# Six or five matmuls a weight tile in an fp32-accurate decoder step, on one Trainium2 core

## The reference, cut to what matters

```python
bg, cg, xv = jnp.split(h @ w_in, 3, axis=-1)              # layer 0: 1024 -> 3*1024
conv, new_hist = causal_dwconv(cg * xv, hist, conv_w)
y = (bg * conv) @ w_out                                   # 1024 -> 1024
...
gconv, new_hist = causal_dwconv(h @ w_gate, hist, conv_w) # ConvFFN of each layer: 1024 -> 2816, twice
y = (jax.nn.silu(gconv + conv_b) * (h @ w_up)) @ w_down   # 2816 -> 1024
...
p = (h @ w_qkv).reshape(b, t, N_GROUPS, 3, H_SLOT, HEAD_DIM)   # layer 1: 1024 -> 4608
```

## Time and profile before

| | |
|---|---|
| three runs | 1483.51, 1487.76, 1491.68 us; median 1487.76 us |
| the profiled execution | 1491.81 us, of which 1490.3 us are the span of the trace |
| granted TensorE clock, mean over the span | 0.962 |
| busy: TensorE, weight loads, VectorE, ScalarE | 95%, 90%, 52%, 33% of the span |
| matmuls | 10995 |

### The profile page before, as it was taken

The page is one execution under the profiler, slowest core; times in us unless marked ns, Lnnn a source line. Parts: engine busy times, 40 slices in busy tenths (PEclk is TensorE's granted clock), DMA queues, the critical chain, the costliest instruction groups (busy, mean ns, idle before and its releaser), DMA issues.

```text
span 1490.3 us, 28043 instructions
## 1 busy us (share of the span) xinstructions
PE 1417.3 (95%) x10995; PEld 1342.2 (90%) x10995; DVE 778.9 (52%) x1236; ACT 487.7 (33%) x779; POOL 21.1 (1%) x50
## 2 busy tenths in 40 slices
PE   5999999999999999999989999776999999999998
PEld 5999999999999999988878888644499999999998
DVE  5655656565565333354454544667176555664223
ACT  3222334343433222333333333211153433332111
POOL 0000000000000000000000000000000000000000
PEclk9999999999999999999999999855899999999999
DMA  5254446544444444451340341397064445345331
GB/s 162 86 173 132 142 140 196 154 153 136 123 150 140 145 149 127 147 161 58 95 152 28 91 125 52 87 248 198 25 196 143 131 125 166 122 132 179 111 95 58
DMA packets 241729, 195.01 MB, mean 131 GB/s; under 512 B 6825, under 2 KB 229081, under 8 KB 240514
## 3 DMA queue, kind: packets, MB, share of 16 engines
q1 hardware_dynamic: 226976, 128.88, 30.9%
q0 software_dynamic: 1792, 54.43, 10.1%
q10 hardware_dynamic: 12906, 10.92, 2.4%
HBM read 186.58 MB, written 65.21 MB: 169 GB/s over the span
## 4 chain that ended last, share of the span: by engine, by line
PE 86%; DVE 5%; issue 3%; ACT 2%; DMA 2%; SPq 1%; ACTq 1%; DVEq 0%
PE acc L1267 74%; PE N L1256 2%; PE M L1432 2%; PE acc L1576 2%; DMA big<-new_q 1%; PE N L1461 1%; PE acc L1295 1%; DVE big L1130 1%; PE M L1256 1%; DVE big L1069 1%; ACT big L732 1%; PE M L1453 1%; PE M L1449 1%; ACT big L719 1%; SPq L458 1%
## 5 line engine op out<-in xcount | busy, mean ns | idle before, releaser
L1267 PE MATMUL acc<-hh,wh 128*128 128x260 f32 x2320 | 480.1, 288 | 1.0 <-issue 1.0
L1267 PE MATMUL acc<-hh,wl 128*128 128x260 f32 x2320 | 467.0, 283 | 0.0
L1267 PE MATMUL acc<-hl,wh 128*128 128x260 f32 x2320 | 466.7, 283 | 0.0
L573 ACT ACTIVATE wh<-wraw 128x1024 fp32r<-128x1024 f32 x212 | 222.8, 1051 | 500.2 <-PE acc L1267 486.2
L1267 PEld LDWEIGHTS acc<-hh,wh 128*128 128x128 f32 x2320 | 359.3, 189 | 7.0 <-issue 1.3
L1267 PEld LDWEIGHTS acc<-hh,wl 128*128 128x128 f32 x2320 | 357.5, 188 | 0.0
L1267 PEld LDWEIGHTS acc<-hl,wh 128*128 128x128 f32 x2320 | 356.9, 188 | 0.0
L857 DVE TENSOR_TENSOR wl<-wraw,wh 128x1024 fp32r<-128x1024 f32 x212 | 257.4, 1214 | 177.1 <-ACT wh L573 168.9
L1267 PE MATMUL acc<-yh,wh 128*128 128x260 f32 x864 | 175.2, 284 | 3.0 <-DVEq L891 2.0
L1267 PE MATMUL acc<-yh,wl 128*128 128x260 f32 x864 | 174.5, 283 | 0.0
L1267 PE MATMUL acc<-yl,wh 128*128 128x260 f32 x864 | 174.2, 283 | 0.0
(11 more groups left out here) (182 smaller groups left out, 1162.1 us busy)
## 6 DMA issues: line engine op xcount, KB each, us to landing
out_dram<-in_cache_kv_d_dram POOLq DMA_DIRECT2D x24, 1364.0 KB, 6.2
wraw<-in_ffn_w_gate_dram SPq DMA_DIRECT2D x44, 512.0 KB, 3.8
wraw<-in_ffn_w_up_dram SPq DMA_DIRECT2D x44, 512.0 KB, 3.9
wraw<-in_attn_w_qkv_dram SPq DMA_DIRECT2D x36, 512.0 KB, 4.8
out_dram<-in_cache_kv_d_dram POOLq DMA_DIRECT2D x8, 2044.0 KB, 8.1
wraw<-in_ffn_w_down_dram SPq DMA_DIRECT2D x32, 448.0 KB, 3.7
wraw<-in_sc_w_in_dram SPq DMA_DIRECT2D x24, 512.0 KB, 3.8
wraw<-in_ffn_w_down_dram SPq DMA_DIRECT2D x16, 512.0 KB, 3.9
```

The source lines that it names most:

```text
L573: nc.scalar.activation(wh[c % 2][:, 0:k], wraw[:, c % 4, 0:k], ACT.Copy).then_inc(hi_done, 1)
L1267: ins = T.matmul(acc[:, par, h2, 0:HALF], w[c % 2][:, k, :], a[:, k0 + k, h2, :], start=(first and k == 0 and n == 0), stop=(last and k == ...
```

## The change

The two halves of tokens become unequal: A has 264 tokens, B has 256. For each weight tile five matmuls stand in place of six: wh·xh and wh·xl over A (264 columns each, both into bank 0), then one of 512 columns in which wh meets the high and the low part of B's activations one behind the other (into bank 1: its columns 0 to 255 collect the high product, 256 to 511 the low one), then wl·xh over A (264) and over B (256, added to columns 0 to 255 of bank 1). For that `hh` and `hl` are laid into one tensor `hhl` [128, 2, 8, 520] and `yh`, `yl` into `yhl`. All columns together stay 1560.

Bank 1 then holds two results for B. At each readout ScalarE copies the second one (256 columns) from PSUM into the new buffer `lo` (`keep_lo`, in `step`, ahead of the split), and VectorE adds it to the first in place in PSUM (`joined`), waits for that addition, and then reads the tile as one run of 520 tokens across the two banks (`tokens`). In S_QKV and the other stages a few readouts that were made for two halves become one of 520.

```diff
+        def tokens(two):
+            return two.rearrange("p h n -> p (h n)")[:, C0:C0 + TT]
...
+            def keep_lo(two, st, it, t):
+                act.wait_ge(acc_free, st.tile(it, t) + 2)
+                nc.scalar.activation(lo[:], two[:, 1, BB:2 * BB], ACT.Copy).then_inc(lo_kept, 1)
...
             def step(st, it, c, last=False):
                 g = st.chunk(it, c)
                 act.wait_ge(chunk_used, g + 1)
+                if st is S_DN0 or st is S_DN1:
+                    if c % 3 == 2:
+                        keep_lo(acc[:, (c // 3) % 2], st, it, c // 3)
+                elif st is S_IN and it == 0 and c == 2:
+                    keep_lo(M[:], st, it, c)
+                else:
+                    keep_lo(acc[:, c % 2], st, it, c)
...
             def finish(pair):
                 act.wait_ge(chunk_used, S_QKV.chunk(pair, 8) + 1)
+                keep_lo(acc[:, 0], S_QKV, pair, 8)
                 split_hi(S_QKV, pair + 1, 0)
...
+            def joined(two, st, it, t):
+                dve.wait_ge(lo_kept, st.tile(it, t) + 1)
+                ch.after(V.tensor_tensor(two[:, 1, 0:BB], two[:, 1, 0:BB], lo[:], ALU.add))
+                return tokens(two)
...
-                V.tensor_tensor(xm, acc[:, par, :, 0:HALF], xm, ALU.add).then_inc(x_ready, 1)
+                V.tensor_tensor(xm, joined(acc[:, par], st, it, m % 4), xm, ALU.add).then_inc(x_ready, 1)
...
-                    V.tensor_tensor(dst, src[:, :, 0:HALF], r[:], ALU.mult).then_inc(acc_free, 1)
+                    V.tensor_tensor(dst, joined(src, S_IN, it, k), r[:], ALU.mult).then_inc(acc_free, 1)
...
-                        V.tensor_tensor(u_prompt, acc[:, 0, :, 0:HP], prompt(r), ALU.mult)
-                        V.tensor_tensor(u_new, acc[:, 0, :, HP:HALF], sample(r), ALU.mult).then_inc(u_ready, 1)
+                        a = joined(acc[:, 0], gu, it, 2 * i)
+                        V.tensor_tensor(u_prompt, prompt(a), prompt(r), ALU.mult)
+                        V.tensor_tensor(u_new, sample(a), sample(r), ALU.mult).then_inc(u_ready, 1)
...
-                        ch.after(V.tensor_tensor(y32[:], acc[:, 1, :, 0:HALF], t1[:], ALU.mult))
+                        ch.after(V.tensor_tensor(y32[:], joined(acc[:, 1], gu, it, 2 * i + 1), t1[:], ALU.mult))
...
-                a = acc[:, c % 2]
+                a = joined(acc[:, c % 2], S_QKV, pair, c)
...
+            def tile_step(dst, w, a, k, first, last):
+                T.matmul(dst[:, 0, C0:512], w[0], a[:, 0, k, 0:BA], start=first, stop=False)
+                T.matmul(dst[:, 0, C0:512], w[0], a[:, 1, k, 0:BA], start=False, stop=False)
+                T.matmul(dst[:, 1, 0:2 * BB].rearrange("p (t n) -> p t n", t=2), w[0], a[:, :, k, BA:TT],
+                         start=first, stop=False)
+                T.matmul(dst[:, 0, C0:512], w[1], a[:, 0, k, 0:BA], start=False, stop=last)
+                return T.matmul(dst[:, 1, 0:BB], w[1], a[:, 0, k, BA:TT], start=False, stop=last)
...
-                    for n, (w, a) in enumerate(((wh, xh), (wh, xl), (wl, xh))):
-                        for h2 in range(2):
-                            ins = T.matmul(acc[:, par, h2, 0:HALF], w[c % 2][:, k, :], a[:, k0 + k, h2, :],
-                                           start=(first and k == 0 and n == 0),
-                                           stop=(last and k == nk - 1 and n == 2))
+                    ins = tile_step(acc[:, par], (wh[c % 2][:, k, :], wl[c % 2][:, k, :]), a, k0 + k,
+                                    first and k == 0, last and k == nk - 1)
```

More of the change, by code:

```diff
@@ L29 @@
 NS = 8
-HALF = 260
-HP = SEQ // 2
-HS = NS // 2
+TT = SEQ + NS
+BB = 256
+BA = TT - BB
+C0 = 512 - BA
 FF = 2816
@@ L1232, in _ @@
                     gained(3, m, m + 3 * DK)
+            ch.end(2)
             ch.begin()
@@ L1236, in _ @@
             ffn(1, S_GU1, S_DN1, DK + FK, 4 * DK, None, 2)
-            for j in range(2):
-                last = V.tensor_copy(xs_c[:, :, j * HS:(j + 1) * HS], x[:, :, j, HP:HALF])
-            last.then_inc(fin_xs, 1)
+            V.tensor_copy(xs_c, x[:, :, SEQ:TT]).then_inc(fin_xs, 1)
             for t in range(4):
@@ L1277, in mean_square @@
                 pe.wait_ge(ssq_ready, (norm + 1) * DK + 1)
-                for h2 in range(2):
-                    ins = T.matmul(N[:, h2, 0:HALF], rms_ones[:], ssq[:, h2, :], start=True, stop=True)
-                ins.then_inc(ms_ready, 1)
+                T.matmul(N[:, 0, C0:512], rms_ones[:], ssq[:, 0:BA], start=True, stop=True)
+                T.matmul(N[:, 1, 0:BB], rms_ones[:], ssq[:, BA:TT], start=True, stop=True).then_inc(ms_ready, 1)
             def first_chunk(norm):
@@ L1288, in first_chunk, with k_step @@
                 return {k: (lambda k=k: at(k)) for k in range(DK)}
-            def k_step(dst, c, k, xh, xl, first, last):
-                for n, (w, a) in enumerate(((wh, xh), (wh, xl), (wl, xh))):
-                    for h2 in range(2):
-                        ins = T.matmul(dst[:, h2, 0:HALF], w[c % 2][:, k, :], a[:, k, h2, :],
-                                       start=(first and n == 0), stop=(last and n == 2))
-                return ins
+            def k_step(dst, c, k, a, first, last):
+                return tile_step(dst, (wh[c % 2][:, k, :], wl[c % 2][:, k, :]), a, k, first, last)
             pe.wait_ge(pool_set, 6)
@@ L1400, in ffn @@
                     free_acc(gu, 0, c)
-                    products(gu, 0, c, c % 2, DK, hh, hl, 0, True, True, first_chunk(norm) if c == 0 else None)
+                    products(gu, 0, c, c % 2, DK, hhl, 0, True, True, first_chunk(norm) if c == 0 else None)
                 with pe.Fori(1, FK // 2) as it:
@@ L1459, in head_sums @@
                 pe.wait_ge(qsq_ready, pair * 6 + (i + 1))
-                for h2 in range(2):
-                    ins = T.matmul(N[:, h2, 0:HALF], head_ones[:], sq[:, h2, :], start=True, stop=True)
-                ins.then_inc(qms_ready, 1)
+                T.matmul(N[:, 0, C0:512], head_ones[:], sq[:, 0:BA], start=True, stop=True)
+                T.matmul(N[:, 1, 0:BB], head_ones[:], sq[:, BA:TT], start=True, stop=True).then_inc(qms_ready, 1)
             def project(pair, attend):
@@ L1498, in project @@
                         pe.wait_ge(kvt_dve, pair * 4)
-                    products(S_QKV, pair, c, c % 2, DK, hh, hl, 0, True, True, ins)
+                    products(S_QKV, pair, c, c % 2, DK, hhl, 0, True, True, ins)
             def finish(pair):
@@ L1590, in _ @@
                     free_acc(S_WO, it, c, d=1 if c == 0 else 2)
-                    products(S_WO, it, c, c % 2, NP_, yh_r, yl_r, 0, True, True)
+                    products(S_WO, it, c, c % 2, NP_, yhl, 0, True, True)
             ffn(1, S_GU1, S_DN1, DK + FK + NP_ + 1, 3)
```

163 lines of the change are left out of this document (80 added, 83 removed).

## The result

The changed kernel took 1498.55 us (median of 13 runs, 1495.53 to 1502.83), the kernel before 1488.53 us (13 runs on the same chip, 1483.51 to 1491.68): a ratio of 1.0072 [1.0058, 1.0086]. It is 10.0 us slower; the forecast was 6.8 us faster. The range held the time, but the direction was the rival's, "the extra goes by column".

What follows compares the result with a forecast made beforehand. TensorE's issue distance, 120.14 ns per matmul start, was taken as the bound. A gain of 17.7 us less 10.9 us of costs made −6.8 us: 1491.81 becomes 1485.0 (1481.0 for the median); range 1462 to 1500.

Steps and rivals of the forecast that it cites:

- the extra goes by column: Rival on TensorE: the extra time goes mostly by column, 2.5 ns saved a tile; +7.1 us, 1494.9; chance 0.22.
- fixed part per instruction: TensorE: each matmul carries 11.8 ns beyond its columns, so five instead of six save 11.8 ns a weight tile.
- the three readings: Why 260 columns take 120.14 ns: fixed per instruction, by column, or weight-load floor; 11.8, 2.5 or 24 ns saved a tile.
- The floor of the load: Rival: the weight load sets the 120 ns, the long matmul costs 216; 24 ns saved a tile, −25 us; chance 0.10.
- the rival of the dearer long matmul: Rival: the 512-column matmul costs 30 ns more than 225, so five lose to six; about 1529 us; chance 0.08.
- Tiles on the path: Of 1632 weight tiles, 1502 count on TensorE's path; at 11.8 ns each, 17.7 us gained.
- The readout: Copy and addition at 180 readouts: 1.14 us later from idle, 0.57 where VectorE is behind; costs sum to 10.9 us.
- S_IN, steady part and start: S_IN: 0.2 us for 7 first chunks of a v, 1.4 in all; at the start the split 0.6 late.
- starts of gate/up, two: Start of gate/up, twice: the split ends 0.3 us late each time, 0.6 in all.
- behind the four pairs (`finish`): TensorE waits for the last chunk's readout: 1.14 us for the first pair, 0.57 for each of three, 2.85 in all.
- S_WO and the pause behind it: S_WO, paced by VectorE: 2.3 us more at the middle wait, 2.0 at the end, 4.3 in all.
- Steady loops: Gate/up and down, 60 chunks twice: a readout shift of 1.1 us is covered, cost 0.

Runs made afterwards that it cites:

- the long operand in one run: Changed kernel, its 512-column matmul reading 512 neighbouring columns instead of two runs of 256, so B's tokens lack their right products: 1493.74 us in one run.
- the packed constant: Kernel before, its four low matmuls per tile reading one small gapless constant bf16 tile, so low products are missing from the result: 1452.85 us in one run.
- the grouped run: Kernel before, low products read as bf16 at a step of two elements, chunks without inserts running all one-pass matmuls first, then bf16: 1465.47 us, 0.9851.
- The experiment with down of layer 0: Changed kernel with six matmuls a tile and no copy or addition in S_WO and in down of layer 0: 1490.89 us, 1.0010.
- the two with six matmuls in S_WO: Changed kernel with six matmuls and no copy or addition in S_WO alone (1491.28 us), or in S_WO and down of layer 0 (1490.89 us).

## Why the prediction was wrong, point by point

**The step that failed is "fixed part per instruction".** It gave each instruction 11.8 ns on top of 260/2.4 and so 11.8 ns saved a tile. The distances of the changed kernel decide between the three readings: 118.6 ns for 256 columns and 232.7 for 512 are 114.1 ns for 256 columns more, 0.446 ns a column, which leaves 4.5 ns fixed. The tile says the same from the other side: one instruction less at equal columns saved 5.0. The fixed part is known only to a few ns, for the distance also depends on the place in the tile: with six matmuls, copy and addition, 256 columns took 118.6 to 120.1 ns. But no stretch of any run gives 11.8: the tile saved 2.4 ns in down, and 7.5 and 7.7 with the long operand in one run. The text had the right reading in hand (0.452 ns a column and 2.5 fixed) and gave it 0.22. Its forecast for that case, 122 and 234, stands against 121 to 122 and 232.7. The floor of the load (216) is out. So is the rival of the dearer long matmul: it costs 8 ns more than the 225 of the forecast, not 30.

Where the argument went astray: at the lower clock nothing stood on top of 260/1.2, and this was read as "start-up or read cost per instruction, and equally a limit of the read rate". It was indeed equal evidence; the choice between the two rested on "a new address pattern and a new weight load come with each instruction", which no row carried. The fp32 rows were the only ones of two lengths, and they gave 2.5 ns fixed.

The Trainium skill (TensorE: Matmul & The Clock Gate, section "Back-to-back issue gap") gives N/2.4 + 2.5 ns, which it calls the gap of an isolated matmul, and about 131 ns for each matmul of 512 columns in a sustained stream. For the one-pass type neither holds here: 512 columns would be 215.8 by the formula and took 232.7; only its small fixed part is near what gate/up showed (4.5 to 5.0). For bf16 the formula gives 110.8 at 260 columns: the packed constant agrees (110.6 and 110.8), the grouped run with its step of two does not (115.6 to 117.4).

**Tiles on the path.** 1502·5.0 = 7.5 us, beside 7.4 and 6.9 measured. In down the tile gave back less, 2.4 ns (718.3 ns against 720.6, averages between 490 and 590 us): there the two matmuls of A with `wh` take 122.7 and 123.3 ns. With 352 such tiles the sum is about 6.6. Why they are dearer stays open; with the long operand in one run they took 120.6 and 121.9.

**The readout.** The prices of the single instructions were right (431 and 380 ns, the wait for the addition 0.16). The places were not. For this the changed kernel is set against the run with five matmuls and no copy and addition, stage by stage, in the starts of the products of the two profiled executions (20.7 us in all; 18.1 by medians):

| place | predicted, us | measured, us |
|---|---|---|
| S_IN, steady part and start | 1.4 + 0.6 | 0.3 |
| starts of gate/up, two | 0.6 | 0.8 + 1.0 |
| start of down, layer 0 | 0 | 0.6 |
| pause before S_QKV | 0 | 1.0 |
| behind the four pairs (`finish`) | 2.85 | 1.6 + 0.5 + 0.5 + 1.6 |
| S_WO and the pause behind it | 4.3 | 4.7 |
| lower clock in S_WO, start and middle | 0 | 1.5 + 2.6 |
| last readout | 1.14 | 0.9 |
| lower clock behind the pause before S_QKV, and in S_OUT | 0 | 1.5 + 1.5 |

What is left (+0.3 within S_QKV, −0.2 before S_IN) nearly cancels. Of the 9.8 us between 10.9 and 20.7, the lower clock is 7.1. The medians say 18.1, so part of that belongs to this execution.

- *Steady loops:* right. No iteration of gate/up or down waits; S_IN has slack where 0.2 a v were counted.
- *Starts of gate/up:* the wait for the third chunk's split came as foreseen (0.3 recorded), but TensorE waits once more at the fourth chunk: 1118.90 and 1125.07 us are the two tiles in layer 1 that are 0.37 and 0.24 longer than without the addition. A shift at a start is handed on to the next chunk.
- *Start of down:* ScalarE's table load and split came 1.8 us later than before (the split of `wh` at 480.14, before at 478.33), and there was less cover than that. The text counted the whole of down at nothing.
- *Pause before S_QKV:* the missing term. `free_acc` of S_QKV's first chunk asks for all earlier tiles, as that of S_WO, which the text had named. So a readout that elsewhere lies behind the other half of `acc` is on the path there, with the full detour of 1.0 (1.14 estimated). The experiment with down of layer 0 gives it back.
- *`finish`:* the middle pairs are as counted (0.5 each, 0.57 predicted); the first cost 1.6 in place of 1.14 and the last 1.6 in place of 0.57. Why was not followed.
- *S_WO:* the middle wait grew somewhat less than predicted, to 3.8 us where 4.3 were forecast. Against the run without the addition the middle costs 1.6 and the end 1.0 us; two waits of 0.8 at ordinary chunk ends, which the text did not count, bring the sum to about its 4.3. The lower clock behind the middle wait, left out of the sum and put at 2 to 3, cost 2.6 us: four tiles are at 1.3 to 1.46 us in place of 0.72 to 0.82, a fifth at 0.94. Another 1.5 us are three tiles at the start of S_WO; the kernel before has these too, so against it they are no loss.
- *The other lower clock, 3.0 us:* in S_OUT (window 181.6 above) the clock fell in three of the five kernels that copy and add there, not in the two with six matmuls in S_WO, whose S_OUT is the same. It also fell there in the kernel with the packed constant (0.50 for 3 us from 178), which has neither copy nor addition. Behind the long pause before S_QKV it fell in two of four. So these 3.0 us are no fixed price of the detour; they belong in part to the execution.

With the measured sizes in the prediction's own sum: −7.5 from the tile and +18.1 from the readout are +10.6, where +10.0 was measured. So the two terms of the sum were the right ones, and both were mis-sized: the gain by 10 us through the failed step, the price by 7 through the seams and the clock. That the time still fell into the range (1462 to 1500) is owed to the rival's case, which set its upper end; the forecast's own range ended at 1487.

## What to carry to other kernels

Before instructions are merged, split their distance into a part per instruction and a part per column, from rows of two lengths in the same type; if the rows have only one length, an argument for the fixed part is worth no more than the other, and the gain is to be taken at the smaller. Work added to a readout was free here in the steady loops and was paid at the seams: wherever a wait asks for all earlier tiles, list every such wait in the code, not only the one that the profile shows as long. TensorE may come back from a long wait at the lower clock: in the middle of S_WO the wait grew by 1.6 us and the clock took another 2.6.

## What the runs showed of the hardware that was not expected

- The one-pass fp32r type does not reach one column a cycle of 2.4 GHz (0.417 ns) in this kernel: 0.446 ns a column plus 4.5 ns, from 118.6 ns for 256 columns and 232.7 for 512.
- Beside the 120.1 ns of the one-pass type, bf16 takes 115.8 ns for 260 columns with a step of two elements and 110.7 packed (there one small tile was read again and again).
- The change from the one-pass type to bf16 costs 10 to 15 ns, packed or not. In every tile it takes most of the gain away (0.9970 of the time before); with most chunks changing once it does not (0.9851).
- A long operand of two runs of 256 columns takes the same time as one of 512 neighbours in gate/up (232.7 and 233.1 ns), but the tile around it took 2.5 ns more, and 5.4 more in down.
- Behind a wait of 3.8 us in the middle of S_WO the clock stood at 0.50 for 5.9 us. Behind waits of 2.2 to 2.3 us at the same place it fell in three kernels and stayed up in three, as in the kernel before after 2.0 us; behind the pause of 2.0 us before S_QKV it fell in two executions of four. What decides is open: these runs differ in more than the wait, and none changed the wait alone.
